# Inverting the chunk triangles of an RWKV-7 recurrence: 32-token diagonal blocks in place of whole 64-token matrices

## The chip, the core and the metric

The kernel runs on one core of a Trainium2 chip. The metric is the device time of one execution in microseconds. The core has a matrix engine (TensorE; the profile writes PE for its products and PEld for its weight loads), a vector engine (VectorE, DVE), a scalar engine (ScalarE, ACT), GpSimd (POOL) and a queue that issues transfers (SyncE, SP). Each works through its own program in order; semaphores join them. Products are written to PSUM, a memory of 128 partitions with banks of 512 float32 columns; everything else lies in SBUF. The array of TensorE can be used as several smaller tiles: the partitions on which a product's operands lie choose a group of rows of the array, those on which its result lies a group of columns.

## What is computed

One layer of a streaming encoder for a prompt of 1024 tokens and a sample of 64 tokens. Each layer has three token mixers (an RWKV-7 recurrence, windowed attention, attention to a memory), gates, an output projection and a gated MLP. The change touches only the recurrence, whose definition for each of 8 heads of width 64 is:

```python
def step(S, inp):
    r_t, w_t, k_t, v_t, kk_t, a_t = inp
    sa = jnp.einsum('bhvk,bhk->bhv', S, -kk_t)
    S = S * w_t[:, :, None, :] + sa[..., None] * (kk_t * a_t)[:, :, None, :] + v_t[..., None] * k_t[:, :, None, :]
    return S, jnp.einsum('bhvk,bhk->bhv', S, r_t)

s_fin, o = lax.scan(step, s0.astype(jnp.float32), (tm(rh), tm(wh), tm(kh), tm(vh), tm(kk), tm(ah)))
```

Taken 64 tokens at a time, the values `sa` of a chunk solve a triangular system: with N the strictly lower triangle of the 64x64 products between the decayed queries and keys of the chunk, the kernel needs the inverse of 1 - N for every head and chunk. There are 17 chunks (16 of the prompt, one of the sample).

## The kernel before

The 1088 tokens are worked through in three groups of 384, 384 and 320 columns. In every group the dense products (projections, gates, branches, MLP) run through one stream of units: SP loads a weight tile, ACT rounds it to `w_hi` (L318), DVE subtracts to get `w_lo` (L473), PE takes three products for each 128x128 piece (L300 to L302). Attention and the recurrence are written as generators of steps, one per engine, and `in_order` weaves them between halves of those units: after each step of the recurrence every engine gets one half of a dense unit, and after some steps none. Of the 36 steps of a group's scan these have no dense work behind them: the second and seventh of the first pair, the third and ninth of the second pair, the fifth of the third pair, and the first of the last state steps. This order is fixed at build time and the same on all engines.

The scan treats chunks in pairs: chunk `u` = 0 lies on partitions 0 to 63, chunk 1 on 64 to 127, and the 8 heads lie side by side in the columns. Groups have three pairs each; the last pair of all has one chunk. While one pair's inverse is made, the state of the pair before is carried on (`state_pe` and its siblings).

The inverse has ten steps (`inverse_pe`, `inverse_act`, `inverse_pool`, `inverse_dve`). D is the part of N inside diagonal blocks of 16 tokens, kept with its transpose; the masks LOW, LOW_T and OFF_T cut D, its transpose and the rest out of the raw products.

1. Second step: `gram` (L1469) makes the key and query products into `px[0]` (128 columns a product) and the transposed ones into `px[1]` (64 columns); DVE masks them into `m2` (L1653), `m1` (L1657), `off_t` (L1659), `mb` (L1662). POOL makes Y = 1 + D transposed (L1616).
2. Third to sixth step: `plain` (L1456) makes D², D⁴ and D⁸, ACT copies them out of PSUM (L1580 to L1593), and Y is multiplied by 1 + D², 1 + D⁴, 1 + D⁸, each time a `plain` and an addition on DVE (L1672, L1676, L1680). Between them stand products of the keys, transposes of tokens (L1477) and L1546. DVE then transposes Y in blocks of 32 (L1682).
3. Seventh step: `plain` makes M, the rest of the triangle times Y; ACT copies it (L1602).
4. Eighth to tenth step: three solves, each a `plain` with M and an addition of Y on DVE (L1686, L1689, L1694): Y + M(Y + M(Y + MY)).

`plain` has one 64x64 product for each head and chunk, so 16 for a full pair; chunk 0 and chunk 1 use different rows and columns of the array. `gram` takes them in the order of `by_parity`, which goes through four combinations of rows and columns.

Of the kernel before, what the change touches and what calls it, by code (L numbers as in the profile page):

```python
# [29 lines left out]
ACT = mybir.ActivationFunctionType  # L30
# [40 lines left out]
LOW, LOW_T, OFF_T, UP, INCL = range(5)  # L71
# [7 lines left out]
H = [slice(0, 64), slice(64, 128)]  # L79

# [1413 lines left out]
def inverse_pe(pe, c, p):  # L1494
    S, px, C = c.S, c.px, CHUNK
    b, w = p % 2, lanes(p)
    ar, at = c.ar, columns_of(p).start
    x0, x1, x2, x3 = px[0][:, 0], px[0][:, 1], px[1][:, 0], px[1][:, 1]
    m1, m2, m3, m4, y = c.m1, c.m2, c.m3, c.m4, c.y
    yield  # L1500
    pe.wait_ge(S["operands"], p + 1)
    if p:
        pe.wait_ge(S["solve_read"], 3 * p)
        pe.wait_ge(S["m_read"], p)
    if p % 3 == 0:
# [3 lines left out]
    if p:
        pe.wait_ge(S["powers_read"], 3 * p)  # L1510
        pe.wait_ge(S["lkv_read"], p)
    gram(pe, px[1], lambda e, j, u: c.a_r[b][H[e], j, u, 0:C], lambda e, j, u: c.b_n[H[e], j, u * C:(u + 1) * C], p,
         C).then_inc(S["low"], 1)
# [27 lines left out]
    plain(pe, x0, m3, y, p).then_inc(S["y_sum"], 1)  # L1541
# [12 lines left out]
    plain(pe, x0, m1, y, p).then_inc(S["solve"], 1)  # L1554
    yield
    pe.wait_ge(S["solve_read"], 3 * p + 1)
    plain(pe, x1, m1, m2, p).then_inc(S["solve"], 1)
    yield
    pe.wait_ge(S["solve_read"], 3 * p + 2)
    plain(pe, x0, m1, m3, p).then_inc(S["solve"], 1)  # L1560
    yield


def inverse_act(act, c, p):
# [15 lines left out]
    act.activation(c.m3[0:w, :, :], heads(px[1][0:w, 0, :]), ACT.Copy)  # L1580
    act.activation(c.m4[0:w, :, :], heads(px[1][0:w, 1, :]), ACT.Copy).then_inc(S["powers_read"], 1)
# [3 lines left out]
    act.activation(c.m1[0:w, :, :], heads(px[1][0:w, 0, :]), ACT.Copy)  # L1585
    act.activation(c.m2[0:w, :, :], heads(px[1][0:w, 1, :]), ACT.Copy).then_inc(S["powers_read"], 1)
# [6 lines left out]
    act.activation(c.m3[0:w, :, :], heads(px[1][0:w, 0, :]), ACT.Copy).then_inc(S["powers_read"], 1)  # L1593
# [8 lines left out]
    act.activation(c.m1[0:w, :, :], heads(px[0][0:w, 1, :]), ACT.Copy).then_inc(S["m_read"], 1)  # L1602
# [6 lines left out]
def inverse_pool(pool, c, p):  # L1609
    S = c.S  # L1610
    b, w, nu = p % 2, lanes(p), len(chunks_of(p))
    yield
    pool.wait_ge(S["low_read"], p + 1)
    if p:
        pool.wait_ge(S["solve_read"], 3 * p)
    pool.tensor_tensor(c.y[0:w], c.m2[0:w], c.ident64[0:w, :].unsqueeze(1).to_broadcast([w, 8, CHUNK]),  # L1616
                       ALU.add).then_inc(S["y1"], 1)
    yield
    pool.wait_ge(S["gram_k"], p + 1)
    for t in (c.b_n, c.k_n):  # L1620
        v = t[:, :, 0:w].rearrange("p j (u t) -> p j u t", u=nu)
# [4 lines left out]

def inverse_dve(dve, c, p):
# [44 lines left out]
    dve.tensor_tensor(flat(y[0:w]), px[0][0:w, 0, :], flat(y[0:w]), ALU.add).then_inc(S["y_added"], 1)  # L1672
# [3 lines left out]
    dve.tensor_tensor(flat(y[0:w]), px[0][0:w, 0, :], flat(y[0:w]), ALU.add).then_inc(S["y_added"], 1)  # L1676
# [412 lines left out]
def allocate(nc, c, k):  # L2089
# [11 lines left out]
    c.tri, c.ident64 = sb(k, "tri", [5, CHUNK]), sb(k, "ident64", [CHUNK])  # L2101
# [27 lines left out]
    with ExitStack() as f:  # L2129
# [26 lines left out]
        c.m1, c.m2, c.m3, c.y = (sb(f, n, [8, C]) for n in ("m1", "m2", "m3", "y"))  # L2156
# [4 lines left out]
        with ExitStack() as s:  # L2161
            c.m4 = sb(s, "m4", [8, C])
# [240 lines left out]
```

## Time and profile before

| | |
|---|---|
| three runs, median | 2161.18 us (2160.21 to 2166.73) |
| profiled execution | 2159.54 us |
| its span, first to last instruction | 2157.7 us |
| PE busy | 2084.4 us (97%) |
| PEld busy | 1997.0 us (93%) |
| DVE busy | 1277.6 us (59%) |
| ACT busy | 907.2 us (42%) |
| POOL busy | 147.7 us (7%) |
| mean granted clock of PE | 0.99 of 2.4 GHz |

Busy time counts an engine as busy while any of its instructions runs; products overlap each other, so a row with several of them is shorter than their number times the mean. A float32 product of the program shows as two matmuls and two weight loads in the trace; one in the rounded format of the dense work shows as one.

### The profile page before, as it was taken

To read this page: it belongs to the slowest core of one execution; us is meant where nothing else is said; L and a number is where in the kernel's file an instruction comes from. 1 tells how busy PE (TensorE), PEld (TensorE's weight loads), DVE (VectorE), ACT (ScalarE), POOL (GpSimd) and SP (SyncE) were. 2 spreads that over 40 slices of the span, in tenths; PEclk is the share of its full clock that TensorE was granted. 3 is DMA by queue.
4 is the path that set the end of the run, shared out by engine and by line. 5 is a ranking of instruction groups with operands and counts; after the bars stand their busy time and mean duration, and the time that the engine had idled before them with its cause. 6 is when DMAs were issued, how large, how long until landed. Compare 5 with 4: busy or idle time off the path is not lost.

```text
span 2157.7 us, 41418 instructions
## 1 busy us (share of the span) xinstructions
PE 2084.4 (97%) x17507; PEld 1997.0 (93%) x17507; DVE 1277.6 (59%) x2100; ACT 907.2 (42%) x1450; POOL 147.7 (7%) x238
## 2 busy tenths in 40 slices
PE   5999999999999999999999999999899999999999
PEld 5899899899999998989989999999798899899999
DVE  6566653656666535674454676654376644577753
ACT  5455333345444334543333544443354333354542
POOL 1000011001111000000000011100000010011110
PEclk9999999999999999999999999999899999999999
DMA  4422211344334452231124444345522212444444
GB/s 162 148 82 79 75 51 60 103 147 125 127 126 159 142 167 69 69 89 56 51 69 141 128 127 128 127 155 152 150 79 74 79 56 82 152 146 149 148 155 134
DMA packets 86248, 243.83 MB, mean 113 GB/s; under 512 B 11312, under 2 KB 24880, under 8 KB 86064
## 3 DMA queue, kind: packets, MB, share of 16 engines
q1 hardware_dynamic: 86064, 241.19, 35.9%
q8 instruction: 139, 2.28, 0.4%
q14 instruction: 45, 0.37, 0.1%
HBM read 235.06 MB, written 6.09 MB: 112 GB/s over the span
## 4 chain that ended last, share of the span: by engine, by line
PE 86%; DVE 6%; ACT 2%; DMA 2%; issue 2%; SPq 1%; DVEq 0%; ACTq 0%
PE sums L300 23%; PE sums L302 22%; PE sums L301 22%; PE px L1456 5%; PE ps_o L1004 2%; DMA raw<-w_branch 1%; DVE w_lo L473 1%; PE ps_t L981 1%; PE px L1469 1%; PE pz L1732 1%; PE ps_s L964 1%; PE ps_s L967 1%; ACT w_hi L318 1%; DMA raw<-w_attn 1%; PE px L1477 1%
## 5 line engine op out<-in xcount | busy, mean ns | idle before, releaser
L300 PE MATMUL sums<-x_hi,w_hi 128*128 128x384 f32 (+1 forms) x2208 | 743.7, 337 | 37.0 <-DVE q L495 15.0
L301 PE MATMUL sums<-x_lo,w_hi 128*128 128x384 f32 (+1 forms) x2208 | 724.9, 328 | 0.0
L302 PE MATMUL sums<-x_hi,w_lo 128*128 128x384 f32 (+1 forms) x2208 | 724.8, 328 | 0.0
L473 DVE TENSOR_TENSOR w_lo<-raw,w_hi 128x1024 fp32r<-128x1024 f32 (+2 forms) x449 | 523.9, 1167 | 313.8 <-ACT w_hi L318 313.4
L318 ACT ACTIVATE w_hi<-raw 128x1024 fp32r<-128x1024 f32 (+1 forms) x452 | 441.0, 977 | 521.4 <-PE sums L302 293.0
L300 PEld LDWEIGHTS sums<-x_hi,w_hi 128*128 128x128 f32 x2208 | 418.5, 190 | 54.5 <-issue 43.5
L301 PEld LDWEIGHTS sums<-x_lo,w_hi 128*128 128x128 f32 x2208 | 419.0, 190 | 1.7
L302 PEld LDWEIGHTS sums<-x_hi,w_lo 128*128 128x128 f32 x2208 | 418.3, 189 | 0.0
L300 PE MATMUL sums<-h_hi,w_hi 128*128 128x384 f32 (+1 forms) x528 | 172.6, 327 | 0.0
L302 PE MATMUL sums<-h_hi,w_lo 128*128 128x384 f32 (+1 forms) x528 | 172.1, 326 | 0.0
L301 PE MATMUL sums<-h_lo,w_hi 128*128 128x384 f32 (+1 forms) x528 | 172.1, 326 | 0.0
L300 PE MATMUL sums<-o_hi,w_hi 128*128 128x384 f32 (+2 forms) x416 | 141.0, 339 | 2.7 <-issue 1.4
L302 PE MATMUL sums<-o_hi,w_lo 128*128 128x384 f32 (+2 forms) x416 | 135.3, 325 | 0.0
L301 PE MATMUL sums<-o_lo,w_hi 128*128 128x384 f32 (+2 forms) x416 | 135.2, 325 | 0.0
L300 PEld LDWEIGHTS sums<-h_hi,w_hi 128*128 128x128 f32 x528 | 99.2, 188 | 0.2
L301 PEld LDWEIGHTS sums<-h_lo,w_hi 128*128 128x128 f32 x528 | 99.1, 188 | 0.2
L302 PEld LDWEIGHTS sums<-h_hi,w_lo 128*128 128x128 f32 x528 | 99.1, 188 | 0.0
L300 PEld LDWEIGHTS sums<-o_hi,w_hi 128*128 128x128 f32 x416 | 78.2, 188 | 6.6 <-issue 3.5
L435 POOL TENSOR_TENSOR h<-h,gl 128x384 f32<-128x384 f32 (+1 forms) x88 | 67.6, 778 | 232.3 <-DVE h L532 200.6
L362 ACT ACTIVATE gl<-cv 128x384 f32<-128x384 f32 (+1 forms) x66 | 33.6, 509 | 116.6 <-DVE cv L567 116.6
L567 DVE SCALAR_TENSOR_TENSOR cv<-a_raw,k_vecs,cv 128x384 f32<-128x384 f32 (+1 forms) x132 | 78.5, 595 | 2.3
L301 PEld LDWEIGHTS sums<-o_lo,w_hi 128*128 128x128 f32 x416 | 78.3, 188 | 1.0
(302 smaller groups left out, 2531.9 us busy)
## 6 DMA issues: line engine op xcount, KB each, us to landing
raw<-w_up SPq DMA_DIRECT2D x132, 512.0 KB, 3.5
raw<-w_gate SPq DMA_DIRECT2D x72, 512.0 KB, 3.6
raw<-w_down SPq DMA_DIRECT2D x48, 512.0 KB, 3.6
raw<-w_rwkv SPq DMA_DIRECT2D x42, 512.0 KB, 3.6
raw<-w_branch SPq DMA_DIRECT2D x72, 256.0 KB, 2.8
raw<-w_attn SPq DMA_DIRECT2D x30, 512.0 KB, 3.7
raw<-w_out SPq DMA_DIRECT2D x24, 512.0 KB, 3.6
raw<-w_down_end SPq DMA_DIRECT2D x24, 384.0 KB, 3.0
```

What stands on the lines that cost most here:

```text
L300: pe.matmul(out, wh[:, ws], n.hi[:, k, :], start=(n.begins and k == 0), stop=False)
L301: pe.matmul(out, wh[:, ws], n.lo[:, k, :], start=False, stop=False)
L302: mm = pe.matmul(out, wl[:, ws], n.hi[:, k, :], start=False, stop=(n.ends and k == n.kt - 1))
L318: act.activation(hi_of(c, u), raw_of(c, u), ACT.Copy).then_inc(S["w_hi"], 1)
L362: act.activation(c.gl[i % 2][:, 0:w], c.cv[i % 2][:, 0:w], ACT.Gelu_apprx_tanh).then_inc(S["gelu"], 1)
L435: ins = pool.tensor_tensor(h[:, tok], h[:, tok], c.gl[i % 2][:, col], ALU.mult)
L473: dve.tensor_tensor(lo_of(c, u), raw_of(c, u), hi_of(c, u).bitcast(F32), ALU.subtract).then_inc(S["w_lo_dve"], 1)
L567: dve.scalar_tensor_tensor(cv, raw[:, tap:tap + w], vec(c, "conv_w", 3 * m + tap), cv, ALU.mult, ALU.add).then_inc(S["conv"], 1)
L964: mm = pe.matmul(c.ps_s[0:p.nq, e, jj * 256 + cols.start:jj * 256 + cols.stop], c.q[H[e], 2 * p.r + jj, tok], c.kw[H[e], at + cols.start:a ...
L967: mm = pe.matmul(c.ps_s[0:p.nq, e, jj * 256:jj * 256 + 256], c.q[:, 4 + 2 * e + jj, tok], c.mk[:, int(p.sample), 2 * e + jj, :], start=Tru ...
L1004: mm = pe.matmul(out, lhs, rhs, start=((n, keys) == p.halves[0]), stop=((n, keys) == p.halves[-1]))
L1456: mm = eng.matmul(out[H[u], h * CHUNK:(h + 1) * CHUNK], tok(lhs, u, h), tok(rhs, u, h), start=True, stop=True)
```

## The change

The diagonal blocks of 16 tokens are kept inside blocks of 32, and only those are computed while powers and Y are made: Y and the powers have 32 columns a head instead of 64, on four blocks of 32 partitions. `odd` and `even` each hold a power and its transpose. The number of factors and their order stay. After Y, M comes from 32-row blocks (`by_blocks`), into both halves of a 64-column head. Then z = (1 + M) Y is made by blocks, with `one_m` from DVE, and the inverse is z + M(Mz) with two calls of `plain`. The transposed products are made for the diagonal blocks alone (`gram_blocks`), twice, once for each orientation, ahead of `gram`; one DVE operation masks both.

```diff
+ROWS = [slice(32 * m, 32 * m + 32) for m in range(4)]
...
+def blocks(p):
+    return [(u, ROWS[2 * u + r], slice(32 * r, 32 * r + 32)) for u in range(len(chunks_of(p))) for r in range(2)]
...
+def diagonal(eng, out, at, lhs, rhs, p):
+    for h in range(8):
+        for _, rows, _ in blocks(p):
+            mm = eng.matmul(out[rows, at + 32 * h:at + 32 * h + 32], lhs[rows, h, :], rhs[rows, h, :], start=True, stop=True)
+    return mm
...
+def by_blocks(eng, out, lhs, rhs, p):
+    for h in range(8):
+        for u, rows, cols in blocks(p):
+            mm = eng.matmul(out[H[u], cols.start // 32, 32 * h:32 * h + 32], lhs[rows, h, :], rhs[rows, h, :],
+                            start=True, stop=True)
+    return mm
...
+def gram_blocks(eng, out, at, lhs, rhs, p):
+    for j in range(4):
+        for u, rows, cols in blocks(p):
+            for e in range(2):
+                n = at + 32 * j
+                mm = eng.matmul(out[rows, e, n:n + 32], lhs(e, j, u, cols), rhs(e, j, u, cols), start=True, stop=True)
+    return mm
...
 def inverse_pe(pe, c, p):
...
+    gram_blocks(pe, px[1], 0, query, key, p)
+    gram_blocks(pe, px[1], 128, key, query, p).then_inc(S["low"], 1)
+    if p:
+        pe.wait_ge(S["solve_read"], 3 * p)
     gram(pe, px[0], ...).then_inc(S["gram_b"], 1)
-    gram(pe, px[1], ...).then_inc(S["low"], 1)
     yield
     pe.wait_ge(S["low_read"], p + 1)
-    plain(pe, x2, m2, m1, p)
-    plain(pe, x3, m1, m2, p).then_inc(S["powers"], 1)
+    diagonal(pe, x2, 0, odd[:, 1], odd[:, 0], p)
+    diagonal(pe, x2, 256, odd[:, 0], odd[:, 1], p).then_inc(S["powers"], 1)
...
     yield
     pe.wait_ge(S["flipped"], p + 1)
-    plain(pe, x1, c.off_t, m4, p).then_inc(S["mprod"], 1)
+    by_blocks(pe, px[0], c.off_t, c.y_t, p).then_inc(S["mprod"], 1)
+    yield
+    pe.wait_ge(S["one_m"], p + 1)
+    pe.wait_ge(S["lkv_read"], p + 1)
+    by_blocks(pe, px[1], c.one_m, y, p).then_inc(S["solve"], 1)
     yield
     pe.wait_ge(S["m_read"], p + 1)
-    plain(pe, x0, m1, y, p).then_inc(S["solve"], 1)
-    yield
     pe.wait_ge(S["solve_read"], 3 * p + 1)
-    plain(pe, x1, m1, m2, p).then_inc(S["solve"], 1)
+    plain(pe, x1, c.m, c.z, p).then_inc(S["solve"], 1)
     yield
     pe.wait_ge(S["solve_read"], 3 * p + 2)
-    plain(pe, x0, m1, m3, p).then_inc(S["solve"], 1)
+    plain(pe, x0, c.m, c.mz, p).then_inc(S["solve"], 1)
...
 def inverse_act(act, c, p):
-    act.activation(c.m3[0:w, :, :], heads(px[1][0:w, 0, :]), ACT.Copy)
-    act.activation(c.m4[0:w, :, :], heads(px[1][0:w, 1, :]), ACT.Copy).then_inc(S["powers_read"], 1)
+    act.activation(halves_of(c.even[0:w]), px[1][0:w, 0, :], ACT.Copy).then_inc(S["powers_read"], 1)
...
     act.wait_ge(S["mprod"], p + 1)
-    act.activation(c.m1[0:w, :, :], heads(px[0][0:w, 1, :]), ACT.Copy).then_inc(S["m_read"], 1)
+    act.wait_ge(S["one_m"], p + 1)
+    act.activation(by_halves(c.m[0:w]), half_heads(px[0][0:w]), ACT.Copy).then_inc(S["m_read"], 1)
...
 def inverse_dve(dve, c, p):
-    dve.tensor_tensor(four(c.m2), view(px[0], first), tri(LOW_T), ALU.mult)
     dve.wait_ge(S["low"], p + 1)
-    dve.tensor_tensor(four(c.m1), px[1][0:w, :, 0:4 * C].rearrange("p e (j t) -> p e j t", j=4), tri(LOW),
-                      ALU.mult).then_inc(S["low_read"], 1)
+    dve.tensor_tensor(c.odd[0:w].rearrange("p n (e j) t -> p n e (j t)", e=2),
+                      px[1][0:w, :, 0:256].rearrange("p e (n x) -> p n e x", n=2),
+                      c.low[0:w].unsqueeze(2).to_broadcast([w, 2, 2, 128]), ALU.mult).then_inc(S["low_read"], 1)
...
-    dve.transpose(flat(c.m4[0:w]), flat(y[0:w])).then_inc(S["flipped"], 1)
+    dve.transpose(flat(c.y_t[0:w]), flat(y[0:w])).then_inc(S["flipped"], 1)
+    yield
+    dve.wait_ge(S["mprod"], p + 1)
+    dve.tensor_tensor(by_halves(c.one_m[0:w]), half_heads(px[0][0:w]),
+                      c.ident64[0:w, :]...to_broadcast([w, 2, 8, 32]), ALU.add).then_inc(S["one_m"], 1)
     yield
     dve.wait_ge(S["solve"], 3 * p + 1)
-    dve.tensor_tensor(flat(c.m2[0:w]), px[0][0:w, 0, :], flat(y[0:w]), ALU.add).then_inc(S["solve_read"], 1)
+    dve.tensor_copy(by_halves(c.z[0:w]), half_heads(px[1][0:w])).then_inc(S["solve_read"], 1)
```

The masks of 16-token blocks that are loaded stay; four more small copies at the start lay them out for the blocks. In the first pair of a group the PE program, at the second and third step, read before (`a_r` and `b_n` are the decayed queries and keys, x16 a number of equal products):

```order
L302 MATMUL sums<-o_hi,w_lo3 128x384
L1469 MATMUL px0<-a_r0,b_n 64x128 x16
L1469 MATMUL px1<-b_n,a_r0 64x64 x16
L1456 MATMUL px1<-m1,m2 64x64 x16
L1456 MATMUL px1<-m2,m1 64x64 x16
L1469 MATMUL px0<-a_r0,k_n 64x128 x16
```

and now:

```order
L303 MATMUL sums<-o_hi,w_lo3 128x384
L1494 MATMUL px1<-b_n,a_r0 32x32 x32
L1494 MATMUL px1<-a_r0,b_n 32x32 x32
L1502 MATMUL px0<-a_r0,b_n 64x128 x16
L1475 MATMUL px1<-odd 32x32 x64
L1502 MATMUL px0<-a_r0,k_n 64x128 x16
```

The transposed products moved ahead of the 128-column ones and became 64 small ones, and 32 products of 64x64 became 64 of 32x32. On DVE in the same place, before (what an instruction waits for stands behind it):

```order
L473 TENSOR_TENSOR w_lo0<-raw0,w_hi1 128x1024 [waits w_hi]
L473 TENSOR_TENSOR w_lo1<-raw1,w_hi2 128x512 [waits w_hi]
L1653 TENSOR_TENSOR m2<-px0,tri 128x512 [waits gram_b]
L1657 TENSOR_TENSOR m1<-px1,tri 128x512 [waits low]
L1659 TENSOR_TENSOR off_t<-px0,tri 128x512
L1662 TENSOR_TENSOR mb0<-px0,tri 128x512
```

and now:

```order
L474 TENSOR_TENSOR w_lo0<-raw0,w_hi1 128x1024 [waits w_hi]
L474 TENSOR_TENSOR w_lo1<-raw1,w_hi2 128x512 [waits w_hi]
L1705 TENSOR_TENSOR odd<-px1,low 128x512 [waits low]
L1709 TENSOR_TENSOR off_t<-px0,tri 128x512 [waits gram_b]
L1712 TENSOR_TENSOR mb0<-px0,tri 128x512
```

One mask stands where two stood, and it waits for the blocks instead of for `gram`. On DVE in the sixth to ninth step, before:

```order
L1680 TENSOR_TENSOR y<-px0,y 128x512 [waits y_added,y_sum]
L1682 STREAM_TRANSPOSE m4<-y 128x512 [waits y_added]
L509 SCALAR_TENSOR_TENSOR merged<-th0,sums 128x384 [waits sum_free0,w_used]
L1686 TENSOR_TENSOR m2<-px0,y 128x512 [waits solve]
L473 TENSOR_TENSOR w_lo0<-raw0,w_hi2 128x1024 [waits w_hi]
L1689 TENSOR_TENSOR m3<-px0,y 128x512 [waits solve]
```

and now:

```order
L1730 TENSOR_TENSOR y<-px0,y 128x256 [waits y_added,y_sum]
L1732 STREAM_TRANSPOSE y_t<-y 128x256 [waits y_added]
L510 SCALAR_TENSOR_TENSOR merged<-th0,sums 128x384 [waits sum_free0,w_used]
L1735 TENSOR_TENSOR even<-px0,ident64 128x2x8x32 [waits mprod]
L1739 COPY z<-px1 128x2x8x32 [waits solve]
L474 TENSOR_TENSOR w_lo0<-raw0,w_hi2 128x1024 [waits w_hi]
L1742 COPY even<-px0 128x512 [waits solve]
```

A new DVE instruction (1 + M, written over `even`) waits for PE between the transpose and the first solve, where DVE had nothing of the inverse before.

## Rows read from the trace of the kernel before

**Rows 1.** The page, part 1: busy us (share of the span) xinstructions.

```profile
PE 2084.4 (97%) x17507; PEld 1997.0 (93%) x17507; DVE 1277.6 (59%) x2100; ACT 907.2 (42%) x1450; POOL 147.7 (7%) x238
```

**Rows 2.** Windows, first and third scan: us, busy by engine, clock, DMA share, GB/s.

```profile
230.00:383.00 153.00, 149.62 (x2636) 139.00 (x2635) 71.28 (x112) 46.57 (x79) 15.48 (x15) 1.00 0.19 58
...
1681.00:1820.00 139.00, 133.42 (x2271) 124.96 (x2270) 66.76 (x111) 44.13 (x77) 13.37 (x14) 1.00 0.21 62
```

**Rows 3.** Windows, first scan, instructions on `px` alone: PE, PEld, DVE, ACT.

```profile
230.00:383.00 153.00, 54.10 (x1572) 49.00 (x1572) 23.77 (x36) 16.94 (x30) 1.00 0.19 58
```

**Rows 4.** Groups by shape, PE: xcount | busy us, mean ns | idle before, releaser.

```profile
L1456 PE MATMUL px<-m 64*64 64x64 f32 x1904 | 69.1, 220 | 4.1 <-DVE m L1657 4.1
...
L1456 PE MATMUL px<-y,m 64*64 64x64 f32 x1088 | 40.6, 220 | 2.1 <-ACT m L1602 2.1
...
L1456 PE MATMUL px<-m,off_t 64*64 64x64 f32 x272 | 10.3, 221 | 0.0
...
L1469 PE MATMUL px<-a_r,b_n 64*64 64x128 f32 x272 | 9.9, 276 | 2.3 <-DVE k_n L1644 2.3
...
L1469 PE MATMUL px<-b_n,a_r 64*64 64x64 f32 x272 | 5.8, 218 | 0.0
```

**Rows 5.** Chain of waits, first pair, sixth step: start us, us on the chain.

```profile
256.85 1.08 PE px L1456 x32
257.93 0.93 PE px L1546 x32
258.86 0.37 PE sums L300
259.23 0.17 PE sums L301
```

**Rows 6.** Chain of waits, a state step on one array tile.

```profile
363.69 1.14 PE pz L1732 x16
```

**Rows 7.** Timeline of PE, first pair, second step: start us, us, xcount.

```profile
237.86 1.10 PE L1469 MATMUL px<-a_r,b_n 64*64 64x128 f32 x32 [0.43 <-DVE k_n L1644]
238.78 0.64 PE L1469 MATMUL px<-b_n,a_r 64*64 64x64 f32 x32
```

**Rows 8.** Timeline of PEld, attention, products with one or two moving columns.

```profile
821.39 0.97 PEld L933 LDWEIGHTS ps_x<-k_ones_head,ar 128*128 128x128 f32 x8 [0.90 <-ACT ar L326]
822.27 0.97 PEld L933 LDWEIGHTS ps_x<-k_ones,ar 128*128 128x128 f32 x8
```

**Rows 9.** Chain of waits, first pair, from the second to the third step.

```profile
237.81 1.74 DVE w_lo L473 x2
239.54 0.60 DVE m L1653
240.15 0.61 DVE m L1657
```

**Rows 10.** Waits of PE and PEld, whole run: total us, times, longest us.

```profile
PE px L1456 <- DVE m L1657: 4.1, 3, 1.4
...
PE px L1456 <- ACT m L1602: 2.1, 3, 0.7
...
PEld px L1546 <- ACT k_tok L1596: 0.7, 3, 0.2
```

**Rows 11.** Groups by shape on DVE, ACT and POOL, in the inverse.

```profile
L1682 DVE STREAM_TRANSPOSE m<-y 128x512 f32<-128x512 f32 x8 | 5.7, 711 | 0.3
L1672 DVE TENSOR_TENSOR y<-px,y 128x512 f32<-128x512 f32 x8 | 5.5, 692 | 24.2 <-PE px L1456 24.2
...
L1602 ACT ACTIVATE m<-px 128x512 f32<-128x512 f32 x8 | 4.8, 598 | 18.4 <-PE px L1456 18.4
...
L1581 ACT ACTIVATE m<-px 128x512 f32<-128x512 f32 x8 | 4.7, 592 | 0.0
...
L1616 POOL TENSOR_TENSOR y<-m,ident 128x512 f32<-128x512 f32 x8 | 10.3, 1282 | 235.3 <-DVE m L1657 235.3
```

More of the change, by code:

```diff
@@ L70 @@
 N_MASKS = 6
-LOW, LOW_T, OFF_T, UP, INCL = range(5)
+OFF_T, UP, INCL = range(3)
 X_B, X_CUM, X_KK = slice(0, 4), slice(4, 8), slice(8, 12)
@@ L1484, in heads, with halves_of, by_halves, half_heads @@
     return t.rearrange("p (h t) -> p h t", h=8)
+def halves_of(t):
+    return t.rearrange("p n h t -> p (n h t)")
+def by_halves(t):
+    return t.rearrange("p h (r t) -> p r h t", r=2)
+def half_heads(t):
+    return t[:, :, 0:256].rearrange("p r (h t) -> p r h t", h=8)
 def flat(t):
@@ L1498, in inverse_pe @@
     x0, x1, x2, x3 = px[0][:, 0], px[0][:, 1], px[1][:, 0], px[1][:, 1]
-    m1, m2, m3, m4, y = c.m1, c.m2, c.m3, c.m4, c.y
+    odd, even, y = c.odd, c.even, c.y
+    key = lambda e, j, u, cols: c.b_n[H[e], j, u * C + cols.start:u * C + cols.stop]
+    query = lambda e, j, u, cols: c.a_r[b][H[e], j, u, cols]
     yield
@@ L1502, in inverse_pe @@
     if p:
-        pe.wait_ge(S["solve_read"], 3 * p)
-        pe.wait_ge(S["m_read"], p)
+        pe.wait_ge(S["powers_read"], 3 * p)
     if p % 3 == 0:
         pe.wait_ge(S["prepped"], p // 3 + 1)
+    if p:
+        pe.wait_ge(S["lkv_read"], p)
+        pe.wait_ge(S["solve_read"], 3 * p - 2)
+    gram_blocks(pe, px[1], 0, query, key, p)
+    gram_blocks(pe, px[1], 128, key, query, p).then_inc(S["low"], 1)
+    if p:
+        pe.wait_ge(S["solve_read"], 3 * p)
     gram(pe, px[0], lambda e, j, u: c.b_n[H[e], j, u * C:(u + 1) * C], lambda e, j, u: c.a_r[b][H[e], j, u, :], p,
          2 * C).then_inc(S["gram_b"], 1)
[L1509 to L1513, printed above, removed]
     yield
     pe.wait_ge(S["low_read"], p + 1)
-    plain(pe, x2, m2, m1, p)
-    plain(pe, x3, m1, m2, p).then_inc(S["powers"], 1)
+    diagonal(pe, x2, 0, odd[:, 1], odd[:, 0], p)
+    diagonal(pe, x2, 256, odd[:, 0], odd[:, 1], p).then_inc(S["powers"], 1)
     pe.wait_ge(S["b_read"], p + 1)
@@ L1522, in inverse_pe @@
     pe.wait_ge(S["powers_read"], 3 * p + 1)
-    plain(pe, x2, m4, m3, p)
-    plain(pe, x3, m3, m4, p).then_inc(S["powers"], 1)
+    diagonal(pe, x2, 0, even[:, 1], even[:, 0], p)
+    diagonal(pe, x2, 256, even[:, 0], even[:, 1], p).then_inc(S["powers"], 1)
     pe.wait_ge(S["k_read"], p + 1)
     pe.wait_ge(S["y1"], p + 1)
-    plain(pe, x0, m3, y, p).then_inc(S["y_sum"], 1)
+    diagonal(pe, x0, 0, even[:, 0], y, p).then_inc(S["y_sum"], 1)
     turn_tokens(pe, c, x1, lambda j: ar[:, X_V.start + j, at:at + w], p).then_inc(S["turned_v"], 1)
@@ L1530, in inverse_pe @@
     pe.wait_ge(S["powers_read"], 3 * p + 2)
-    plain(pe, x2, m2, m1, p).then_inc(S["powers"], 1)
+    diagonal(pe, x2, 0, odd[:, 1], odd[:, 0], p).then_inc(S["powers"], 1)
     pe.wait_ge(S["y_added"], 3 * p + 1)
-    plain(pe, x0, m1, y, p).then_inc(S["y_sum"], 1)
+    diagonal(pe, x0, 0, odd[:, 0], y, p).then_inc(S["y_sum"], 1)
     pe.wait_ge(S["hats"], p + 1)
     pe.wait_ge(S["v_in"], p + 1)
+    if p:
+        pe.wait_ge(S["lkv_read"], p)
     turn_tokens(pe, c, x1, lambda j: c.b_n[:, j, 0:w], p)
@@ L1540, in inverse_pe @@
     pe.wait_ge(S["y_added"], 3 * p + 2)
-    plain(pe, x0, m3, y, p).then_inc(S["y_sum"], 1)
+    diagonal(pe, x0, 0, even[:, 0], y, p).then_inc(S["y_sum"], 1)
     pe.wait_ge(S["bk_read"], p + 1)
@@ L1571, in inverse_act @@
         act.wait_ge(S["operands"], p)
-        act.wait_ge(S["mprod"], p)
+        act.wait_ge(S["solve"], 3 * p - 2)
     act.activation(c.ep[:, :, 0:nu, 1:C + 1], c.ar[:, X_CUM, cw].rearrange("p j (u t) -> p j u t", u=nu), ACT.Exp)
@@ L1584, in inverse_act @@
     act.wait_ge(S["y1"], p + 1)
-    act.activation(c.m1[0:w, :, :], heads(px[1][0:w, 0, :]), ACT.Copy)
-    act.activation(c.m2[0:w, :, :], heads(px[1][0:w, 1, :]), ACT.Copy).then_inc(S["powers_read"], 1)
+    act.activation(halves_of(c.odd[0:w]), px[1][0:w, 0, :], ACT.Copy).then_inc(S["powers_read"], 1)
     act.wait_ge(S["turned_v"], p + 1)
@@ L1592, in inverse_act @@
     act.wait_ge(S["powers"], 3 * p + 3)
-    act.activation(c.m3[0:w, :, :], heads(px[1][0:w, 0, :]), ACT.Copy).then_inc(S["powers_read"], 1)
+    act.wait_ge(S["y_sum"], 3 * p + 1)
+    act.activation(flat(c.even[0:w, 0]), px[1][0:w, 0, 0:256], ACT.Copy).then_inc(S["powers_read"], 1)
     act.wait_ge(S["turned_bk"], p + 1)
@@ L1671, in inverse_dve @@
     dve.wait_ge(S["y_sum"], 3 * p + 1)
-    dve.tensor_tensor(flat(y[0:w]), px[0][0:w, 0, :], flat(y[0:w]), ALU.add).then_inc(S["y_added"], 1)
+    dve.tensor_tensor(flat(y[0:w]), px[0][0:w, 0, 0:256], flat(y[0:w]), ALU.add).then_inc(S["y_added"], 1)
     yield
@@ L1675, in inverse_dve @@
     dve.wait_ge(S["y_added"], 3 * p + 1)
[L1676 removed]
+    dve.tensor_tensor(flat(y[0:w]), px[0][0:w, 0, 0:256], flat(y[0:w]), ALU.add).then_inc(S["y_added"], 1)
     yield
@@ L1979, in start_dve @@
         dve.tensor_copy(c.ident64[rows, :], c.ident[rows, rows])
-        for dst, src in ((LOW, BD_LOW), (LOW_T, BD_LOW_T), (OFF_T, BD_OFF_T), (UP, BD_UP)):
+        for dst, src in ((OFF_T, BD_OFF_T), (UP, BD_UP)):
             dve.tensor_copy(c.tri[rows, dst], c.masks[rows, src, rows])
+    for q in ROWS:
+        dve.tensor_copy(c.low[q].rearrange("p n (j t) -> p n j t", j=4),
+                        c.masks[q, BD_LOW:BD_LOW_T + 1, q].unsqueeze(2).to_broadcast([32, 2, 4, 32]))
+        dve.tensor_copy(c.ident32[q, :], c.ident[q, q])
     dve.tensor_copy(c.tri[:, INCL], c.masks[:, UP_INCL, 0:CHUNK])
@@ L2100, in allocate @@
     c.lora = sb(k, "k_lora", [2, 512])
-    c.tri, c.ident64 = sb(k, "tri", [5, CHUNK]), sb(k, "ident64", [CHUNK])
+    c.tri, c.ident64 = sb(k, "tri", [3, CHUNK]), sb(k, "ident64", [CHUNK])
+    c.low, c.ident32 = sb(k, "low", [2, 128]), sb(k, "ident32", [32])
     c.state = [sb(k, f"state{s}", [4, CHUNK]) for s in range(2)]
@@ L2155, in allocate @@
         c.b_n, c.k_n = sb(f, "b_n", [4, 2 * C]), sb(f, "k_n", [4, 2 * C])
-        c.m1, c.m2, c.m3, c.y = (sb(f, n, [8, C]) for n in ("m1", "m2", "m3", "y"))
+        c.odd, c.even, c.z = sb(f, "odd", [2, 8, 32]), sb(f, "even", [2, 8, 32]), sb(f, "z", [8, C])
         with ExitStack() as s:
@@ L2161, in allocate @@
         with ExitStack() as s:
-            c.m4 = sb(s, "m4", [8, C])
+            c.y, c.y_t = sb(s, "y", [8, 32]), sb(s, "y_t", [8, 32])
         c.en = sb(f, "en", [4, 2 * C])
@@ L2170, in allocate @@
     c.mg_hi, c.mg_lo = c.o_hi, c.o_lo
+    c.m, c.one_m = (t[:, :, :, :].rearrange("p n h t -> p (n h t)").rearrange("p (h t) -> p h t", h=8) for t in (c.odd, c.even))
+    c.mz = c.one_m
     c.q_sq, c.k_raw, c.k_sq = c.ar[:, 14:22, :], c.ar[:, 22, :], c.ar[:, 23, :]
```

16 lines of the change are left out of this document (8 added, 8 removed).

## The prediction

> **What bounds the kernel now.** I read the busy times first: PE is busy 97% of the span, DVE 59%, ACT 42% [rows 1]. Busy PE could still mean slow or waiting PE, so next I took the three stretches in which the recurrence runs, one per token group [rows 2]: the granted clock is 1.00 there (the upper level, 2.4 GHz), PE is busy 149.62 of 153.00 us in the first, and DVE 71.28 and ACT 46.57. The share of it that writes `px`, the tile of the inverse, is 54.10 us [rows 3]. The waits confirm it: over the whole run PE waits 4.1 us for the masked triangles and 2.1 us for the copy of M [rows 10]. The dense products that are woven between the steps hide the other engines. So PE time in the inverse is span, and the change is priced as PE time; what is saved on DVE, ACT and POOL is worth only what it takes off those few waits.
>
> **The unit of price.** One float32 product of the program is two entries of the trace: the line of `plain` has 1904+1088+272 entries [rows 4], which is 12 calls on 8 full pairs of chunks (16 products each) and one half pair (8), times two. What one entry costs depends on how many array tiles run beside each other, and four rows show it:
> - `plain`, two tiles of 64x64 (one per chunk): a second call of the same shape behind a first takes 0.93 us for 32 entries [rows 5], 29 ns each, so a tile gives one every 58 ns.
> - One tile alone: 16 entries in 1.14 us [rows 6], less one matmul's own 0.22 us [rows 4], over 15: 61 ns.
> - `gram` with 64 moving columns in the order of `by_parity`, four tiles: 32 entries in 0.64 us [rows 7], less 0.22 us, over 31: 13.6 ns, a tile every 54 ns. So four tiles do run at once.
> - `gram` with 128 columns: 1.10 us, less its own 0.27, over 31: 26.8 ns, a tile every 107 ns [rows 7]. Loading 128 weight columns for one or two moving columns takes 0.88 us per 8 [rows 8], 110 ns.
>
> A tile's time is thus set by the larger of its moving and its weight columns: 58 ns at 64, 107 to 110 at 128, about 0.79 ns a column plus 7. No row has 32. My estimate from this line is 32 ns for a 32x32 tile; with four tiles at once (four row groups and four column groups, as `gram` has four pairs) an entry costs 8 ns.
>
> **The change part by part**, for a full pair of chunks.
> - Removed on PE: 12 calls of `plain` at 0.93 us and the 64-column `gram` at 32 x 13.6 ns = 0.44 us: 11.60 us.
> - Eight calls of `diagonal` (five powers, three products with Y), 32 products or 64 entries each: 512 x 8 ns = 4.10 us.
> - `gram_blocks` twice: 128 entries of 32 columns on eight tiles (two row groups by four column groups). Four at a time is what a row shows: 128 x 8 = 1.02 us.
> - `by_blocks` twice: 128 entries on four tiles, but its weights have 64 columns, so 58/4 = 14.5 ns: 1.86 us.
> - Two `plain` stay: 1.86 us.
> - Three more changes of tile shape (blocks to `gram` in the first step, `diagonal` to `gram` in the second, `diagonal` to the 64x64 product L1546 in the fifth). The chain prices one: the first call of 32 after dense work takes 1.08 instead of 0.93, and the first dense product after it 0.37 instead of 0.17 [rows 5]. I take 0.17 each, 0.50.
> - Sum 9.34 us against 11.60: **2.26 us less**, eight times 18.1 us. In the half pair `plain` runs on one tile and still costs 0.93 (16 x 58), while `diagonal` has 32 entries on two tiles, 16 ns each: 8.8 against 11.6, 2.8 less. Together **20.9 us**.
>
> Waits. In the first pair of each group no dense work stands between the first and the second step. There PE now waits 1.4 us [rows 10]: DVE does two weight splits to 239.54, then the two masks one after the other, 0.60 and 0.61 us [rows 9]. After the change one mask of the same 512 columns serves both triangles, and it needs only the blocks, which go ahead of `gram`. DVE would still begin at 239.54 and end near 240.15; PE is ready at 237.86 + 1.02 + 0.15 + 0.88 = 239.9. The wait becomes 0.3: 1.1 us gained three times, 3.3. The opposite happens at two places. Behind the sixth step (the first pair of each group again) PE waits 2.1 us in three places for ACT's copy of M, 0.60 us [rows 10, 11]; it will wait for DVE's sum 1+M, about 0.69 by the row of an addition of that size [rows 11], 0.1 more each: 0.3. ACT's copy of M now waits for DVE too, and the next weight split is queued behind it on ACT, as is one behind the sum on DVE; both belong to units two further on, and dense halves lie between. In the fifth step of the third pair, where PE waits 0.7 us in three places for ACT's copies of the turned keys [rows 10], PE arrives 0.42 earlier (0.51 instead of 0.93 before it): 1.3 lost. Net of waits **1.7 us gained**.
>
> At no cost: halved additions and transpose on DVE (0.69 and 0.71 each for 512 columns), one ACT copy where two of 0.60 stood, POOL's first Y at half of its 1.28 us [rows 11], and four more small copies at the start; PE is not waiting for any of these.
>
> Total 20.9 + 1.7 = 22.6 us. From the profiled execution's 2159.54 us that gives 2136.9; the median of the runs lies 1.6 us above that execution, so **2138.5 us**.
>
> **A rule of the Trainium skill against it.** The row shows 58 ns at 64 columns and 107 at 128 [rows 5, 7], so a tile still gains from 128 to 64. "TensorEngine Tiling (Array Packing)", Performance Considerations, Instruction Overhead, says that a matmul has an overhead of some 60 cycles, that one of a single column lasts as long as one of 60, and that no tiling factor should be taken from a dimension that is already small. By this page 32 columns would cost a tile about what 64 cost, and the sum would be the first rival's. The trace neither confirms nor refutes it below 64. The page's Gotcha 1 says that different row tiles cannot use the same PSUM bank at the same time; here the trace disagrees for two: both halves of `plain` write one bank on different partitions and run two at a time, 29 instead of 61 ns. For four in a bank it has no row; that is the second rival.
>
> **The rivals.**
> - *Small tiles cost what large ones cost* (slower). A 32x32 entry keeps its tile for 58 ns, so that with four tiles `diagonal` and `gram_blocks` pay 14.5 ns: 640 x 14.5 + 1.86 + 1.86 + 0.50 = 13.5 us, 1.9 more than before, in the half pair 0.95 more, 16.2 in all, less 1.4 of waits: 2176 us. It decides from (11.60 - 4.22)/640 = 11.5 ns an entry, 46 ns a tile; above that the change loses. For it: no row below 64 columns. Against: the line through 64 and 128 has a small constant.
> - *Four writers in one bank go two at a time* (slower). `gram`, the one row with four tiles at once, writes two banks; `diagonal` writes one. Then 512 x 16 = 8.2 us, 13.4 in all, 1.8 more per full pair, 2.8 less in the half pair: 2172 us. Against: `plain` shares a bank freely.
> - *Part of it is given back* (no change). Either entries settle at 10 to 11.5 ns, because no row shows a longer stretch faster than 13.6, or PE, now quicker between steps, waits at the six places of a group where no dense work stands; at one DVE operation plus its signal, 0.9 us each, 18 of them are 16 us. 2151 to 2166 us.
> - *More than forecast.* `by_blocks` isn't held by its 64 weight columns (8 ns: 0.83 less a pair) and `gram_blocks` runs eight tiles at once (0.5 less): 12 us more, 2127 us.
>
> **How the numbers follow.** Forecast 0.62, small tiles 0.11, bank 0.06, given back 0.12, more 0.09. Around the forecast an entry between 6.8 (half of the 13.6) and 9 ns is worth 7 us, tile changes 2, waits 3: its own range is 2130 to 2148. To hold 8 in 10 the range takes in the better case and the one that gives part back: 2127 to 2166. A measurement of this kernel can tell about 0.3%, 6.5 us, from no change: faster (below 2154.7) 0.71, within it 0.12, slower (above 2167.7) 0.17.
>
> **What would show it.** In the profile after, a `diagonal` call of 64 entries should take about 0.5 us behind another; 0.93 is the first rival, 1.0 the second (then `gram_blocks`, on two banks, would stay at 0.5 a call). `by_blocks` should take 0.93. PE's time on `px` in the first stretch should fall from 54 to about 47 us, its wait for the mask to 0.3 us in three places, and a wait for 1+M of 0.7 to 0.8 us should appear in three places. The forecast is wrong if an entry costs over 11.5 ns, or if new waits of PE in the three stretches exceed 16 us.

## The result: slower by two per cent, and what the profile shows after

The changed kernel takes 2210.61 us (median of four runs) against 2160.69 us before: the ratio is 1.0204, with a 95% interval of 1.0161 to 1.0246. (One of the four runs took 9693 us for a reason that no trace shows; the ratio leaves it out, and the median of the other three is 2205.66.) So it is slower beyond its interval, though whether by more or less than 2% is not settled. The forecast was 2138.5 us, so it missed by 72 us and on the wrong side. The profiled execution took 2205.66 us with a span of 2203.8, where before had 2157.7.

First the place. Measured from its first gram product to its last state product, a recurrence takes 157.0, 159.6 and 136.0 us in the three groups, and took 142.9, 142.8 and 124.0: 42.9 us more. The other 3.2 of the 46.1 us lie outside. So the loss is where the change is. Part 1 of the page after, which answers to [rows 1], has 3536 more matmul entries on PE than before:

```profile
PE 2100.7 (95%) x21043; PEld 2006.4 (91%) x21043; DVE 1269.2 (58%) x2104; ACT 896.8 (41%) x1432; POOL 142.7 (6%) x238
```

The windows after, as in [rows 2] (us; busy by PE, PEld, DVE, ACT, POOL; granted clock; DMA share; GB/s), first the two that stand there, then the three recurrences from end to end:

```profile
230.00:383.00 153.00, 139.80 (x3650) 127.34 (x3649) 64.83 (x106) 39.62 (x68) 12.29 (x14) 0.93 0.18 55
1681.00:1820.00 139.00, 125.60 (x2770) 114.30 (x2769) 72.81 (x129) 42.89 (x73) 9.75 (x14) 0.93 0.22 67
...
237.00:398.00 161.00, 147.80 (x3849) 134.66 (x3848) 63.98 (x105) 41.42 (x72) 13.82 (x15) 0.94 0.16 52
979.00:1142.00 163.00, 148.89 (x3847) 135.93 (x3845) 63.24 (x105) 41.16 (x71) 13.81 (x15) 0.93 0.17 51
1717.00:1857.00 140.00, 126.09 (x3241) 115.88 (x3242) 57.20 (x100) 37.47 (x67) 11.42 (x14) 0.93 0.18 54
```

PE's time on `px` in the first stretch, the answer to [rows 3], is 51.22 us, where 54.10 stood and about 47 was forecast:

```profile
230.00:383.00 153.00, 51.22 (x2820) 0.93 0.18 55
```

Two things are new. PE is idle for 13 of 153 us, where it was for 3.4. And the granted clock is 0.93 or 0.94, where it was 1.00. A mean of 0.93 between the two levels 2.4 and 1.2 GHz says that 14% of the stretch ran at the lower one; for the three stretches together that is 2 x (161 x 0.06 + 163 x 0.07 + 140 x 0.07) = 62 us.

Now the idle time. PE's waits over the whole run (engine, tile, line, what was waited for: total us, times, longest us), which answer to [rows 10]:

```profile
PE px L1475 <- issue: 18.8, 15, 2.3
PE px L1502 <- issue: 6.9, 4, 2.0
PE px L1510 <- issue: 3.9, 1, 3.9
PE px L1483 <- DVE even L1735: 2.4, 3, 0.8
...
PE pz L1799 <- issue: 1.0, 1, 1.0
```

The wait for the masked triangles is gone (0.3 us in three places were forecast to be left), and the one for 1 + M is 0.8 us in three places, as forecast. But "issue" is new in the recurrences: PE stands still, and no engine, semaphore or transfer of data that the profile shows is what it waits for. With three shorter rows of the same kind this is 32.7 us in 25 places. (Two more places, 1.4 us, lie outside the recurrences, as they did before.) The timeline of PE in the first pair shows where it falls (start us, us, xcount, in brackets the idle time before):

```profile
241.57 1.10 PE L1502 MATMUL px<-a_r,b_n 64*64 64x128 f32 x32
242.68 0.75 PE L1475 MATMUL px<-odd 32*32 32x32 f32 x65
245.14 0.74 PE L1475 MATMUL px<-odd 32*32 32x32 f32 x63 [1.71 <-issue]
...
249.13 1.29 PE L1475 MATMUL px<-even 32*32 32x32 f32 x128
250.27 0.38 PE L1475 MATMUL px<-y,even 32*32 32x32 f32 x20
252.72 0.58 PE L1475 MATMUL px<-y,even 32*32 32x32 f32 x44 [2.08 <-issue]
...
265.10 1.13 PE L1483 MATMUL px<-y_t,off_t 32*64 32x32 f32 x64
```

The small products themselves are quick: 65 entries in 0.75 us, and 128 in 1.29. Less one matmul's own 0.2 that is 8.6 ns an entry. Then PE stops in the middle of a call, behind the 65th entry and behind the 148th (128 + 20), where the program has no wait at all.

What stands at those places is the end of a block of instructions. The queues in part 3 of the page, before and after (packets, MB, share):

```profile
q8 instruction: 139, 2.28, 0.4%
```

```profile
q8 instruction: 166, 2.72, 0.5%
```

A packet has 16.4 KB. Each entry is two instructions of PE, the weight load and the product: 2 x 21043 are 42086, 254 for each packet, and before 252. So queue q8 brings PE's program in blocks of about 256 instructions, 128 entries. Between the two stops above PE did 63 + 32 (gram) + 12 (dense) + 148 = 255 entries and two semaphore instructions, together 512: two blocks. Counted from the start of the trace, the instruction behind each of the 25 stops with "issue" in the recurrences has the same remainder of 256, 193 or 194. In the trace the packet behind the first stop ended at 243.87 us and PE went on at 245.14; behind the second, 251.36 and 252.72. **The theory** is therefore: in a burst of very short products PE uses up its program faster than it arrives, and the clock falls in such stretches. (The clock's record has nine falls in the three recurrences: eight begin in a stop or within 2 us of its end, and one, 3.4 us long, behind two calls of `by_blocks` with the 0.8 us wait for 1 + M between them.) **The rival**: the small tiles bring the stops or the clock by themselves, by their shape.

### The profile page after: what moved, and what is told of

Its sections match the earlier page's. It is cut to its first block, busy times and chain, and to the rows that moved or that the text cites. A ratio compares the mean times of both kernels' runs of the same rounds, so it can differ in the third digit from the quotient of the medians.

```text
span 2203.8 us, 48503 instructions
## 1 busy us (share of the span) xinstructions
PE 2100.7 (95%) x21043; PEld 2006.4 (91%) x21043; DVE 1269.2 (58%) x2104; ACT 896.8 (41%) x1432; POOL 142.7 (6%) x238
## 4 chain that ended last, share of the span: by engine, by line
PE 85%; DVE 6%; issue 4%; DMA 2%; ACT 2%; SPq 1%; DVEq 0%; ACTq 0%
PE sums L301 23%; PE sums L303 22%; PE sums L302 22%; PE px L1475 2%; PE ps_o L1005 2%; DMA raw<-w_branch 1%; PE px L1502 1%; PE ps_t L982 1%; PE px L1483 1%; PE px L1457 1%; DVE w_lo L474 1%; PE pz L1786 1%; PE ps_s L968 1%; PE ps_s L965 1%; PE px L1510 1%
## 5 line engine op out<-in xcount | busy, mean ns | idle before, releaser
L302 PEld LDWEIGHTS sums<-x_lo,w_hi 128*128 128x128 f32 x2208 | 423.6, 192 | 3.0 <-issue 1.3
```

What stands on the lines that cost most here:

```text
L302: pe.matmul(out, wh[:, ws], n.lo[:, k, :], start=False, stop=False)
```

## Experiment 1: the same columns in half the instructions

```diff
-    for h in range(8):
+    for h in range(0, 8, 2):
         for _, rows, _ in blocks(p):
-            mm = eng.matmul(out[rows, at + 32 * h:at + 32 * h + 32], lhs[rows, h, :], rhs[rows, h, :], ...)
+            mm = eng.matmul(out[rows, at + 32 * h:at + 32 * h + 64], lhs[rows, h, :], rhs[rows, h:h + 2, :], ...)
```

> Every product of a diagonal call takes the weights of one head and streams the columns of two, so a call has 16 products of 64 columns where it had 32 of 32; the columns that TensorE streams are the same, the matmul entries fall from 21043 to about 18870 and the packets of the instruction queue from 166 to about 148. (The odd heads are multiplied by their neighbour's block: this part of the inverse is left out; it changes no time by itself.) Theory 'instruction supply' (PE stops because the next 256 instructions, 128 entries, have not arrived; about 33 us in the three stretches, and the clock falls behind such stops): most stops go, under 10 us stay, the granted clock of the stretches is back at 0.97 or more, and the time is 2150 to 2172 us. Rival 'small tiles' (32-row tiles themselves bring the stops or the lower clock): stops and clock stay, 2203 to 2213 us.

Measured: 2148.94 us, 0.9921 of before (0.9897 to 0.9946). Its issue waits, its instruction packets and its first recurrence:

```profile
PE px L1502 <- issue: 3.5, 3, 1.7
...
PE px L1494 <- issue: 0.7, 2, 0.4
PE px L1475 <- issue: 0.4, 1, 0.4
```

```profile
q8 instruction: 149, 2.44, 0.5%
```

```profile
235.00:375.00 140.00, 136.18 (x3081) 123.87 (x3080) 63.79 (x105) 41.50 (x72) 13.79 (x15) 1.00 0.19 59
```

With the tiles as they were and 2176 entries fewer, 2.8% of the time before went (1.0204 to 0.9921), 61 us: the stops fell from 32.7 to 4.6 us and the clock was back at 1.00, 1.00 and 0.99 in the three recurrences. The rival's 2203 to 2213 is out. PE's time on `px` in this stretch is 46.1 us, against 51.2 in the changed kernel and 54.1 before [rows 3].

## Experiment 2: a burst without small tiles

```diff
-    gram(pe, px[1], ..., C).then_inc(S["low"], 1)
+    for _ in range(9):
+        mm = gram(pe, px[1], ..., C)
+    mm.then_inc(S["low"], 1)
```

> The kernel before, with its 64-column gram product issued nine times in a row instead of once (the same result written again). No tile has 32 rows or columns. By the row of that product, 13.6 ns an entry with four tiles, 2176 more entries are 30 us of array time: 2191 us if nothing else happens. Theory 'instruction supply': an entry at 13.6 ns is faster than the 29 ns (3.7 us for 128) that the packets of the kernel after allow in a burst, so the first two steps, 416 entries, run dry: PE stops with nothing to wait for, about 2 us once or twice for each pair, 17 to 35 us, and the granted clock falls in the stretches as in the kernel after: 2212 to 2240 us. Rival 'small tiles': no stops, clock 1.00, 2188 to 2196 us.

Measured: 2209.15 us, 1.0218 of before (1.0180 to 1.0256), 47 us more by that ratio, of which some 30 to 32 are the array's: an entry takes 13.6 ns in a short call and 14.7 in these long ones (128 in 2.09 us, less one matmul's own 0.22). The timeline of one pair in the second group, and the first recurrence:

```profile
1072.58 2.04 PE L1469 MATMUL px<-b_n,a_r 64*64 64x64 f32 x127
1075.40 2.09 PE L1469 MATMUL px<-b_n,a_r 64*64 64x64 f32 x128 [0.79 <-issue]
1078.87 0.70 PE L1469 MATMUL px<-b_n,a_r 64*64 64x64 f32 x33 [1.38 <-issue]
```

```profile
235.00:398.00 163.00, 155.89 (x3370) 144.77 (x3369) 67.22 (x105) 45.09 (x78) 15.49 (x15) 1.00 0.16 51
```

The stops come without any small tile, and exactly 128 entries lie between two of them, 3.47 us from start to start. They sum to 12.4 us in ten places, less than the 17 to 35 expected, so the time fell just short of the expected range (and well above the rival's 2188 to 2196). The other half of the expectation was wrong: the clock did not fall. Stops alone do not explain it.

## Experiment 3: the rate of the supply, with large tiles, small tiles and long entries

Three kernels put one long burst into the first pair of each group. In the first, the 64-column gram of the kernel before is issued 34 times (four 64x64 tiles). The second and third stand on the kernel of experiment 4. Each was run once, so their traces are read and not their times.

```diff
-    gram(pe, px[1], ..., C).then_inc(S["low"], 1)
+    for _ in range(34 if p % 3 == 0 else 1):
+        mm = gram(pe, px[1], ..., C)
+    mm.then_inc(S["low"], 1)
```

> The kernel before, with its 64-column gram product (four tiles of 64x64, 13.6 ns an entry) issued 34 times in a row in the first pair of each group, 1088 entries, the same result written again. Theory 'instruction supply': after a first run of up to two blocks, PE does 128 entries in 1.75 us, stops, and starts the next 128 about 3.5 us after the last (27 ns an entry, as in the two stops of nine_grams that follow each other): 6 or 7 stops of 1.4 to 1.8 us in each burst, each exactly 128 entries behind the other, and about 27 us for a burst where the array needs 14.8. Rival: the stops come from something at the places where they stood (waits, tile changes), none inside this burst, 14.8 us. On the clock: if the stops alone bring it down, it falls to the lower level in or behind all three bursts; if small tiles are needed for that, it stays at the upper level.

```diff
-    diagonal(pe, x2, 0, odd[:, 1], odd[:, 0], p).then_inc(S["powers"], 1)
+    for _ in range(17 if p % 3 == 0 else 1):
+        mm = diagonal(pe, x2, 0, odd[:, 1], odd[:, 0], p)
+    mm.then_inc(S["powers"], 1)
```

> dve_turns, with the first diagonal product of the first pair of each group issued 17 times in a row, 1088 entries of 32x32 tiles, the same result written again. Theory 'instruction supply': the supply doesn't depend on the tile, so again about 3.5 us for each 128 entries, of which PE works 1.1 and stops 2.4; about 27 us for a burst where the array needs 9.4. If the supply were set by the array's own speed, an entry would keep 8.6 ns. On the clock: both views expect it to fall here; beside burst_large it tells whether small tiles are needed for that.

```diff
+    for _ in range(40 if p % 3 == 0 else 0):
+        for h in (0, 4):
+            for _, rows, _ in blocks(p):
+                pe.matmul(x2[rows, 32 * h:32 * h + 128], odd[rows, 1, h, :], odd[rows, 0, h:h + 4, :], ...)
     diagonal(pe, x2, 0, odd[:, 1], odd[:, 0], p).then_inc(S["powers"], 1)
```

> dve_turns, with 640 more entries ahead of the first diagonal product of the first pair of each group: 32x32 weights as there, but each streams 128 columns (four heads; written again by the right product after it). By the 128-column rows of the kernel before, a tile takes 107 to 110 ns for such an entry, so four tiles give one each 27 ns, 3.5 us for 128, which is about what the supply gives (3.45 to 3.73 us in the two bursts). So hardly a stop, at most 0.3 us at a block's end, and some 17 to 18.5 us for a burst. On the clock: if small tiles alone bring it down, it falls to 1.2 GHz in the bursts as in burst_small; if it takes small tiles and stops together, it stays at the upper level, as in burst_large.

Measured, the timeline of PE in the first burst of each, and a window over it. Large tiles:

```profile
246.00 2.09 PE L1469 MATMUL px<-b_n,a_r 64*64 64x64 f32 x128 [1.36 <-issue]
249.46 2.09 PE L1469 MATMUL px<-b_n,a_r 64*64 64x64 f32 x128 [1.36 <-issue]
253.19 2.09 PE L1469 MATMUL px<-b_n,a_r 64*64 64x64 f32 x128 [1.64 <-issue]
```

```profile
240.00:272.00 32.00, 20.55 (x1099) 19.27 (x1090) 3.04 (x5) 2.03 (x3) 2.37 (x3) 1.00 0.02 5
```

Small tiles:

```profile
242.52 1.27 PE L1475 MATMUL px<-odd 32*32 32x32 f32 x128 [0.91 <-issue]
246.53 1.93 PE L1475 MATMUL px<-odd 32*32 32x32 f32 x128 [2.73 <-issue]
249.98 1.93 PE L1475 MATMUL px<-odd 32*32 32x32 f32 x128 [1.52 <-issue]
253.43 1.93 PE L1475 MATMUL px<-odd 32*32 32x32 f32 x128 [1.52 <-issue]
```

```profile
240.00:272.00 32.00, 18.33 (x1124) 16.95 (x1125) 3.04 (x6) 1.33 (x2) 1.83 (x3) 0.57 0.02 4
```

Small tiles with 128 columns an entry:

```profile
240.96 17.67 PE L1567 MATMUL px<-odd 32*32 32x128 f32 x640 [0.76 <-DVE odd L1712]
```

```profile
241.00:258.00 17.00, 17.00 (x624) 17.00 (x628) 1.08 (x2) 0.00 (x0) 0.72 (x1) 1.00 0.02 4
...
979.00:996.00 17.00, 17.00 (x627) 17.00 (x631) 1.03 (x2) 0.00 (x0) 0.66 (x1) 1.00 0.02 4
```

The first two tell the rate: 3.45 to 3.73 us for each 128 entries in the first group, and 3.45 to 4.02 over all six bursts, whatever the tile and whatever the clock. In the first burst of large tiles the longer periods go with packets of q8 that took 1.23 to 1.36 us in place of 0.88 to 0.93; in the later ones not always. That is 27 to 31 ns an entry. The stops stand inside one uniform call, 128 entries apart, so the rival that they come from waits or changes of tile is out. An entry that takes as long by itself, 27.3 ns in the third, runs 640 times without one stop, in all three groups (in the third, a stop of 1.10 us comes in the short products right behind).

They also show what the clock did. With stops between large tiles the same window over the three bursts has 1.00, 0.98 and 1.00 (one fall of 3.4 us, at the end of the second). Small tiles without a stop have 1.00 in all three. Small tiles with stops have 0.57, 0.63 and 0.54: in the first burst the lower level comes 4.2 us after it began and stays for 27 us, and a block takes 1.93 instead of 1.27 us from then on. So in these three runs it fell far only where short small products and stops came together. That doesn't single out the tile's shape: a block of large tiles keeps PE busy for 2.09 us of each period and one of small tiles for 1.27, and no run separates the two.

## Experiment 4: fewer instructions, same result

DVE makes the transposes of D, D² and D⁴, in blocks of 32 (the expectation calls D "M"); TensorE makes only the straight ones. One call of `gram_blocks` and two of `diagonal` go, 192 entries a pair.

```diff
-    gram_blocks(pe, px[1], 0, query, key, p)
-    gram_blocks(pe, px[1], 128, key, query, p).then_inc(S["low"], 1)
+    gram_blocks(pe, px[1], 0, query, key, p).then_inc(S["low"], 1)
...
-    diagonal(pe, x2, 0, odd[:, 1], odd[:, 0], p)
-    diagonal(pe, x2, 256, odd[:, 0], odd[:, 1], p).then_inc(S["powers"], 1)
+    diagonal(pe, x2, 0, odd[:, 1], odd[:, 0], p).then_inc(S["powers"], 1)
...
+    dve.transpose(flat(c.even[0:w, 1]), flat(c.even[0:w, 0])).then_inc(S["turned_p"], 1)
```

> The kernel after, with the transposes of M and of its first two powers made by DVE (blocks of 32) instead of by TensorE: one gram_blocks call and two diagonal calls fewer in a pair, 192 entries, 1.65 us of array time, 14 us in all; entries 21043 to about 19410, packets 154. Theory 'instruction supply': the stops fall from 33 to under 15 us and the clock recovers by half: 2155 to 2180 us, about the kernel before. Rival 'small tiles': only the work goes, plus up to 0.5 us of wait for DVE's transpose at the second step of each group's first pair: 2196 to 2202 us.

Measured: 2146.21 us, 0.9915 of before (0.9889 to 0.9941). Run again:

> dve_turns once more, with more rounds, since its gain over the kernel before is under a per cent. By its first runs 0.988 to 0.995 of the kernel before: 2140 to 2155 us.

Measured: 2143.26 us, 0.9917 (0.9900 to 0.9933). This version beats both kernels, the one before by 0.8% and the changed one by 2.8% (0.9917 against 1.0204). The first recurrence and two of the largest waits of PE on `px` in its first profile:

```profile
235.00:376.00 141.00, 135.57 (x3276) 123.85 (x3275) 66.91 (x116) 40.47 (x72) 13.81 (x15) 0.99 0.19 59
```

```profile
PE px L1475 <- issue: 3.8, 6, 1.0
...
PE px L1475 <- DVE odd L1708: 2.3, 3, 0.8
```

The work that goes is 14 us (192 entries at 8.6 ns on 8.5 pairs); the time fell by 2.9% of that before, 62 us. The rest is stops (5.6 us are left of the 32.7) and clock (0.99, and 1.00 in all three recurrences of the second profile). It came out faster than the 2155 expected: the stops fell well below the 15 us expected, and the clock recovered nearly whole and not by half.

## Experiment 5: the same instructions, dealt out otherwise

```diff
-RECURRENCE_HALVES = PREP_STEPS * [1] + [2] + even(SCAN_STEPS - 1, 29) + [1, 1, 2, 1, 1, 1]
+BY_COUNT = [1, 1, 2, 1, 1, 0, 1, 1, 0] + 2 * [0, 1, 1, 2, 1, 1, 0, 1, 1, 0] + [1, 1, 1, 1, 1, 0]
+RECURRENCE_HALVES = PREP_STEPS * [1] + [2] + BY_COUNT + [1, 1, 2, 1, 1, 1]
```

> The kernel after, with the 29 dense halves of a recurrence dealt out by the number of small products: two behind the fourth step of a pair, one behind its gram step, none behind the last solve and between the later ones. The instructions are the same ones. Theory 'instruction supply': the bursts are thinner, PE's stops fall from 33 to 15 to 25 us, the later solves wait 5 us more for DVE, and the clock recovers in part: 2185 to 2203 us. Rival 'small tiles': the stops do not depend on what lies between, 2211 us plus up to 5 of waits.

Measured: 2215.12 us, 1.0249 of before (1.0181 to 1.0317). No gain over the changed kernel, so the time of the forecast was wrong. The waits say why:

```profile
PE px L1494 <- DVE k_n L1696: 11.6, 9, 1.9
PE px L1475 <- issue: 10.8, 7, 3.5
PE pz L1781 <- issue: 7.7, 8, 1.0
PE px L1483 <- DVE even L1735: 7.3, 9, 0.8
```

The stops at the ends of blocks did fall, from 32.7 to 22 us, as far as expected. But a dense half that stands in the burst is missing elsewhere. PE now waits 11.6 us for DVE's keys (2.3 in the changed kernel), 7.3 for 1 + M (2.4), and 7.7 in eight places behind the last solve, of which seven are not at a block's end: 22 us more, where the expectation had 5. What PE waits for in those eight places no trace shows. The clock did recover in part (0.95, 0.93 and 0.98 in the three recurrences).

## Why the prediction was wrong

**The price of an entry was right.** 8 ns were forecast and 8.6 measured, some 3 us over the run; `by_blocks` takes 1.13 us (the last row of that timeline): 64 entries at 14.5 ns and one matmul's own 0.2, as in the sum. This refutes the rival of small tiles that cost what large ones cost (11.5 ns was its point): with four at once a tile takes 34 ns at 32 columns, where it takes 58 at 64. Read as a tile's price, as it was weighed there, the rule of the Trainium skill ("TensorEngine Tiling (Array Packing)", Performance Considerations, Instruction Overhead) does not hold in this kernel. The rival of the shared bank falls with the same 8.6 ns: four row groups wrote one bank, and it had 16 ns. So does the better case: `by_blocks` costs its 14.5 ns, and the 128 entries of `gram_blocks` took 1.29 us, 8.6 ns each. PE's time on `px` still fell only to 51.2 us and not to 47; 1.2 us of that are the 8.6 ns, and the rest, at stops and at the lower clock, is not split further. (The sum's half pair also leaves out its 0.50 of tile changes, too little to matter.)

**The waits that were priced came as priced**: none for the mask (0.3 in three places expected), 0.8 us in three places for 1 + M, and 1.0 us for the keys where up to 2.0 were expected.

**The step that failed** is the one from entries to time. "So PE time in the inverse is span, and the change is priced as PE time" holds only while PE has its program. The sum priced the small entries at 8 or 14.5 ns each, 3536 more of them in all than before, and put nothing for bringing their instructions that fast. `plain` hid this, because its 29 ns an entry [rows 5] is about the rate of the supply (27 to 31 ns, experiment 3): before, no call of two tiles could outrun it. The prediction came near in one place, the third rival: "no row shows a longer stretch faster than 13.6". It took that for a doubt about the array, and priced it at 10 to 11.5 ns an entry; in a long burst the figure is 27 to 31. Its own sign of a wrong forecast, new waits of more than 16 us in the three stretches, is what appeared: 32.7.

**The second failed term** is the clock, which [rows 2] gave as 1.00 and which the sum took as fixed. By the estimate above, 62 us at half the clock cost up to 31. Why it falls is not shown.

By estimate the parts close: the 22.6 us forecast as gain, less the 3 us above, against 32.7 of stops and at most 31 of clock give up to 44 us more; the three recurrences took 42.9 more. What the lower clock cost was not measured by itself.

The page "Runtime: NRT & Kernel Launch" of the Trainium skill, Instruction fetch mechanics, says that an engine's program arrives in 16 KiB blocks of 256 instructions, which the trace bears out, and that this is hidden because the engine dispatches more slowly than the blocks arrive. Here the measurement differs: PE did 256 instructions in 1.1 to 1.9 us (128 entries at 8.6 or 14.7 ns) and got 256 in 3.45 to 4.02.

**Open**: what sets the 3.5 to 4 us. The packet itself takes 0.9 to 1.4 of it and PE goes on 1.1 to 1.6 us behind its end; whether the rest is the request or something else isn't shown by a trace. Other transfers don't hold it up there: the DMA share in the windows over the bursts is 0.02. Nor is it known what brings the clock down: `dve_turns` has three short falls, each behind the two `by_blocks` calls of a group's first pair, where PE waits for DVE and not for instructions, and the second profile of the same kernel has none.

## What to carry to other kernels

Price a change that makes products smaller twice, by the array's time and by the number of instructions: a burst of more than one or two blocks pays 27 to 31 ns for each weight load and product here, however short they are. Look at the instruction queue's packets before and after, and count entries between two stops without a releaser; 128 says that the program is late. If small tiles are worth having, win them by fewer instructions (more columns for one set of weights, transposes on an idle engine), not by cutting the same columns finer.

## What the runs showed that was not expected

- PE's program is supplied at one block of 256 instructions each 3.45 to 4.02 us in a burst, for 64x64 and 32x32 tiles alike.
- Stops of 0.9 to 1.9 us between large tiles hardly moved the granted clock (0.98 to 1.00), and 17.67 us of small tiles without a stop not at all. With short small products and stops together it was 0.54 to 0.63 over 32 us.
- Work off PE can be worth several times its own time: 14 us of products less gave 62 us, since the stops and the lower clock went with them.
